# Token axis of 640 columns in place of 644, and the side taps of two convolutions in two parts

## The reference, cut to what matters

```python
def _dwconv3(u, w):
    up = jnp.pad(u, ((0, 0), (1, 1), (0, 0)))
    return up[:, :-2] * w[0] + up[:, 1:-1] * w[1] + up[:, 2:] * w[2]

def layer(l, x, cvec, ctx_kv, ang):
    h = _rmsnorm(x, norm1_g[l]) * (1 + sc1) + sh1
    q, k, v, bg, cg, xc = jnp.split(h @ w_in[l], SPLITS, axis=-1)
    ...
    y = _rmsnorm(bg * _dwconv3(cg * xc, conv_w[l]), conv_norm_g[l])
    x = x + g1 * (jnp.concatenate([o, y], axis=-1) @ w_out[l])
    h2 = _rmsnorm(x, norm2_g[l]) * (1 + sc2) + sh2
    a, b = jnp.split(_dwconv3(h2 @ w_up[l], ffn_conv_w[l]), 2, axis=-1)
    x = x + g2 * ((jax.nn.silu(a) * b) @ w_down[l])
    return x, k, v
```

## Time and profile before

| | |
|---|---|
| median of 3 runs | 1607.59 us (1606.13 to 1608.79) |
| the profiled execution's own time | 1607.43 us |
| its span, first to last instruction | 1604.9 us |
| mean granted TensorE clock | 0.989 of full speed |
| PE busy | 1563.9 us, 97% |
| DVE busy | 1029.3 us, 64% |
| ACT busy | 726.9 us, 45% |
| matmuls | 10543 |

### The profile page before, as it was taken

The page is one execution under the profiler, slowest core; times in us unless marked ns, Lnnn a source line. Parts: engine busy times, 40 slices in busy tenths (PEclk is TensorE's granted clock), DMA queues, the critical chain, the costliest instruction groups (busy, mean ns, idle before and its releaser), DMA issues. The chain is left out here.

```text
span 1604.9 us, 26306 instructions
## 1 busy us (share of the span) xinstructions
PE 1563.9 (97%) x10543; PEld 1460.1 (91%) x10543; DVE 1029.3 (64%) x1654; ACT 726.9 (45%) x1214; POOL 150.2 (9%) x174
## 2 busy tenths in 40 slices
PE   5999999999999999999989999999999999999998
PEld 4777888988999999999977788899899999999998
DVE  5672666746775865757775537576587667476673
ACT  3533454326652633526443335443465355253451
POOL 0000000002211202112000000000121120120110
PEclk9999999999999999999989999999999999999999
DMA  9555010474766947769543531034268585694862
GB/s 351 187 178 177 27 53 27 158 249 113 179 148 161 213 127 181 168 154 224 159 138 112 172 105 53 27 105 129 70 148 188 138 192 149 155 206 139 183 157 82
DMA packets 284570, 236.11 MB, mean 147 GB/s; under 512 B 10464, under 2 KB 254752, under 8 KB 284448
## 3 DMA queue, kind: packets, MB, share of 16 engines
q1 hardware_dynamic: 259920, 189.82, 37.8%
q0 software_dynamic: 23680, 44.05, 16.0%
q10 hardware_dynamic: 848, 0.56, 0.1%
HBM read 188.78 MB, written 3.67 MB: 120 GB/s over the span
## 5 line engine op out<-in xcount | busy, mean ns | idle before, releaser
L1541 ACT ACTIVATE w_hi<-raw_all 128x1024 fp32r<-128x1024 f32 x120 | 126.1, 1056 | 227.1 <-DMA raw_all<-raw_all 111.4
L1159 PE MATMUL ps<-gg,w_hi 128*128 128x322 f32 x704 | 219.1, 311 | 0.0
L1161 PE MATMUL ps<-gg,w_lo 128*128 128x322 f32 x704 | 218.7, 311 | 0.0
L1160 PE MATMUL ps<-gg,w_hi 128*128 128x322 f32 x704 | 218.4, 310 | 0.0
L2080 DVE TENSOR_TENSOR w_lo<-raw_all,w_hi 128x1024 fp32r<-128x1024 f32 x120 | 146.5, 1221 | 103.3 <-ACT w_hi L1541 102.3
L1102 PE MATMUL ps<-hc_hi,w_hi 128*128 128x322 f32 x640 | 198.9, 311 | 2.0 <-DVE ub L2103 2.0
L1104 PE MATMUL ps<-hc_lo,w_hi 128*128 128x322 f32 x640 | 199.6, 312 | 0.0
L1106 PE MATMUL ps<-hc_hi,w_lo 128*128 128x322 f32 x640 | 198.9, 311 | 0.0
L636 POOL DMA_DIRECT2D raw_all<-raw_all x160 | 136.3, 869 | 643.5 <-DMA raw_all<-in_w_up_dram 511.2
L1102 PE MATMUL ps<-ht_hi,w_hi 128*128 128x322 f32 x480 | 150.5, 314 | 3.6 <-ACT s L1559 3.5
L1975 DVE SCALAR_TENSOR_TENSOR x<-ps,modv,x 128x128 f32<-128x128 f32 (+2 forms) x240 | 90.3, 433 | 93.0 <-PE ps L1161 54.1
(11 more groups left out here) (210 smaller groups left out, 3464.0 us busy)
## 6 DMA issues: line engine op xcount, KB each, us to landing
raw_all<-in_w_up_dram SPq DMA_DIRECT2D x280, 256.0 KB, 3.8
raw_all<-raw_all POOLq DMA_DIRECT2D x160, 256.0 KB, 4.0
raw_all<-in_w_in_dram SPq DMA_DIRECT2D x48, 512.0 KB, 4.9
raw_all<-in_w_mod_dram SPq DMA_DIRECT2D x48, 512.0 KB, 4.5
raw_all<-in_w_down_dram SPq DMA_DIRECT2D x16, 768.0 KB, 4.4
raw_all<-in_w_down_dram SPq DMA_DIRECT2D x16, 640.0 KB, 4.2
mod_q<-in_w_mod_dram SPq DMA_DIRECT2D x8, 1024.0 KB, 9.4
raw_all<-in_w_out_dram SPq DMA_DIRECT2D x16, 512.0 KB, 4.3
```

What stands on the lines that cost most here:

```text
L1159: mm(out, wh[:, k, :], gh, start=k == 0, stop=False)
L1160: mm(out, wh[:, k, :], gl, start=False, stop=False)
L1161: ins = mm(out, wl[:, k, :], gh, start=False, stop=k == kf - 1)
L1541: A(whi_b[:, 2 * i:2 * (i + 1), :], src, ACT.Copy).then_inc(up_hi[i], 1)
```

## The change

T becomes 640 and HALF 320; the prompt has columns 0 to 127, the sample 128 to 639. No column is padding, so nothing is zeroed. The side taps may no longer reach over a sequence's end: each is issued as two instructions, one over the 127 inner columns of the prompt and one over the 511 inner columns of the sample.

```diff
-T = 644
+T = 640
 HALF = T // 2
-C_PROMPT, C_SAMPLE = 1, 130
+C_PROMPT, C_SAMPLE = 0, 128
+TAP_PARTS = [(C_PROMPT, SEQ - 1), (C_SAMPLE, DEC - 1)]
...
-            for a, e in ((0, 1), (C_SAMPLE - 1, C_SAMPLE), (T - 2, T)):
-                V.memset(x[:, :, a:e], 0.0)
...
-                for buf in (h_hi, h_lo):
-                    for a, e in ((0, 1), (C_SAMPLE - 1, C_SAMPLE), (T - 2, T)):
-                        V.memset(buf[:, :, a:e].bitcast(F32), 0.0)
...
-                        for j, off in ((0, 0), (2, 2)):
+                        for j, off in ((0, 0), (2, 1)):
                             dve.drain()
-                            V.scalar_tensor_tensor(out=tap[:, tile, 1:T - 1], in0=z[:, off:off + T - 2],
-                                                   scalar=cw(j), in1=tap[:, tile, 1:T - 1], op0=ALU.mult, op1=ALU.add)
+                            for c0, n in TAP_PARTS:
+                                a = c0 + 1 - off
+                                V.scalar_tensor_tensor(out=tap[:, tile, a:a + n], in0=z[:, c0 + off:c0 + off + n],
+                                                       scalar=cw(j), in1=tap[:, tile, a:a + n], op0=ALU.mult,
+                                                       op1=ALU.add)
...
-                V.memset(ps[:, B_RMS[2][0], 0:130:129], 0.0)
-                V.memset(ps[:, B_RMS[2][1], 320:322], 0.0)
...
-                    return V.scalar_tensor_tensor(out=cen[:, s, 1:T - 1], in0=u[:, s, j:j + T - 2],
-                                                  scalar=vecs[:, l, w:w + 1], in1=cen[:, s, 1:T - 1], op0=ALU.mult,
-                                                  op1=ALU.add)
+                    for c0, n in TAP_PARTS:
+                        a, b = c0 + 1 - j // 2, c0 + j // 2
+                        ins = V.scalar_tensor_tensor(out=cen[:, s, a:a + n], in0=u[:, s, b:b + n],
+                                                     scalar=vecs[:, l, w:w + 1], in1=cen[:, s, a:a + n], op0=ALU.mult,
+                                                     op1=ALU.add)
+                    return ins
```

## The result

| | before | after |
|---|---|---|
| median | 1607.53 us (13 runs, 1604.59 to 1609.88) | 1612.42 us (13 runs, 1605.48 to 1616.98) |
| profiled execution, its span | 1607.43, 1604.9 us | 1612.64, 1610.8 us |
| mean granted clock | 0.989 | 0.986 |

The ratio is 1.0026, with a 95% interval of 1.0016 to 1.0037: slower by 4.9 us, where 1604.4 and a range up to 1608.5 were forecast. The runs of after also lie further apart than those of before.

What follows compares the result with a forecast made beforehand. PE bounds the kernel through matmul count and pace. The terms -6.8 + 1.4 + 1.7 + 0.4 + 0.5 - 0.2 = -3.0 us, from 1607.43, gave 1604.4 us, with a range of 1599.5 to 1608.5.

Steps and rivals of the forecast that it cites:

- Two columns less per matmul: 7776 matmuls on PE, two columns shorter at 0.438 ns a column: 6.8 us won, bounds 6.5 and 7.2.
- The alignment rival: Row halves starting at multiples of 64 bytes make each matmul 3.6 ns shorter, 28 us in all, 1583 us; chance 0.05.
- Where that gain is not kept: At seven PE waits for snapshot s1, the gain of preceding gates is waited away: 1.4 us lost, between 0 and 2.1.
- The taps in two parts: DVE's side taps cost about 0.12 us more each, 23 us in all, mostly beside PE; it counts at four places.
- SP's block load behind `up_split_lo(g, 3)`: SP's queue waits on this DVE split before loading a later gate's block; delay behind the taps costed at nothing.
- DVE pushes the weight pipeline: Rival: the block loaded behind `up_split_lo(g, 3)` becomes what sums wait for; 6 to 11 us lost, 1609 to 1614; chance 0.10.
- Its sign in the profile: A pushed pipeline would show as ACT's DMA-sum waits growing over some 0.3 us in each third and later gate of a chunk.
- Late gates (u2): In seven late MLP gates, split taps delay snapshot u2 and PE stands still 0.3 us each: 1.7 us lost, bounds 0 and 3.
- The last gate of the chunks of five: The gated product's last low part comes about 0.1 us late, two chunks a layer: 0.4 us lost, between 0 and 0.6.
- The attention round behind the last tap: Behind the convolution group's side taps, PE's wait for probabilities grows 0.24 us, in two layers 0.5 us; bounds 0 and 1.
- The memsets: Removed zeroing on norm 1 buffers, accumulator and x, some 0.06 us each: nothing taken, at most 0.5 us won.

Runs made afterwards that it cites:

- The series of widths: Kernel before with down-projection matmuls cut by output block to 322, 322, 320, 318, 316, 304, 288 and 256 columns, addresses kept: 1595.05 us.
- The dummies: Kernel before plus two unused 62-column DVE instructions in 32 gates, ahead of `up_split_lo(g, 3)`: 1613.09 us; or behind it: 1607.5 us.
- the one with the split between the taps: Changed kernel, tensors padded to old addresses, `up_split_lo(g, 3)` moved between left and right taps in all but a chunk's first gate: 1604.95 us.
- one tap: Each tap one instruction; at 640 columns it runs across the seam between sequences: 1605.14 us at the new addresses, 1597.36 us at the old ones.
- the two runs that differ in the pads' place: Changed kernel with 128 unused bytes behind x only: 1606.41 us; with raw_all, w_hi, w_lo at changed addresses and everything behind at old ones: 1615.25 us.
- the run with pads: Changed kernel, taps in two parts, with an unused tensor behind each shortened one so every tensor keeps its old address: 1605.68 us, 0.999.
- the version with the moved split: Changed kernel with pads, the value half's last right tap put behind `up_split_lo(g, 3)` in all but a chunk's first gate: 1597.23 us, 0.9943.

## Why the prediction was wrong, by its steps

- *Two columns less per matmul*: right in kind, half the size. The term was -6.8 us with bounds of 6.5 and 7.2; the starts came 1.67 ns closer, 13 us. The series of widths gives 0.45 ns a column, the prediction's price. But rows seem to be paid by groups of 16 bytes, four columns each, and the change takes away a whole group in either half: four times 0.45 are 1.8 ns. The alignment rival had the right mechanism with too high a price (3.6 ns, 28 us). The evidence against it, equal halves at 322 columns, did not speak against it: both halves touch 81 groups.
- *Where that gain is not kept*: 1.4 us forecast, bounds 0 and 2.1. With the other two causes taken out 13 us became 10.1 by medians and 8.5 by the ratio, so about 3 to 5 us were waited away: mis-sized.
- *The taps in two parts*: exact as a cost of DVE (347 and 746 ns, eight parts in 3.78 us, 0.47 us a gate). What failed is the step that costed SP's block load behind `up_split_lo(g, 3)` at nothing. This is the rival "DVE pushes the weight pipeline", given a chance of 0.10. The dummies show the channel: 0.39 us a gate ahead of that split cost 4.9 us, behind it nothing. The taps in two parts cost 7.5 us at 644 columns and 7.3 to 8.3 at 640, so the split carries much of it, and u2 (next point) is the candidate for the rest. The argument against the rival was that PE showed only seven waits in 40 gates, so that the pipeline had reserve. PE's few waits say that it had been in time, not by how much. The prediction never measured the slack of that split. Its sign in the profile was badly chosen as well: ACT's waits for DMA sums fell, from 111.4 to 102.1 us, and over all runs but the one with the split between the taps (69.0) they lie anywhere between 82.6 and 123.1 without following the time. SP's wait for the split, 49.0 to 56.7 us, was the line to watch: it is 56.6 to 57.5 in every kernel with the MLP's taps in two parts and the split in its old place, 48.2 to 49.6 in the others that leave the split where it was, but 55.4 with the dummies ahead of it.
- *Late gates (u2)*, +1.7 us, bounds 0 and 3: the mechanism was right and too small. The list of waits has no u2 in after, but the starts show 18 late gates and 4.9 us (0.27 each, where 0.3 was forecast, in seven gates). Such stops stand in every trace with the MLP's taps in two parts, at least 10 of them, and in none with one tap, the two with dummies included. How much of them reaches the end is not shown, since a stop here shortens the next wait for s1. At 644 columns the taps in two parts cost 2.6 us more than the dummies, by medians, and their trace has 2.8 us of stops at u2.
- *The last gate of the chunks of five*, +0.4: borne out. In after, the matmul that needs the last low part starts at 692.61 and takes 0.41 us instead of 0.31, and the next one starts at 692.86, 0.10 us late. Four such places, 0.4 us together, stand in after and none in before; again the list of waits leaves them out.
- *The attention round behind the last tap*, +0.5, bounds 0 and 1: the wait shows (1.2 us in 4 times for the probabilities, 0.3 in one before), and the group takes some 1 us longer in each layer. A size too small, and within the noise of the medians.
- *The memsets*: nothing speaks for more than the nothing taken.
- *What no step had*: the shorter x moves all that is allocated behind it, and raw_all left its 256-byte boundary. This costs 4.6 us at 644 columns (ratio 1.0026) and 6.7 to 8.8 at 640 (8.8 between the two runs that differ in the pads' place, 1606.4 and 1615.3).

The account: -13 us of matmuls, +3 waited away, +8.3 for the two parts, +6.7 for the address, together +5.0; measured +4.9. This is a way to share out the difference, no test of it: -10.1 (the first two terms), +8.3 and +6.7 are the steps between four medians that begin with before and end with after, so they must add up. What tests it are the pairs that do the same thing elsewhere, and they agree within 2 to 4 us. With either cost alone the change would have been about as fast as the kernel before (1605.7 and 1605.1, ratios 0.999 and 0.9988). That the run with pads lies within the forecast's range is luck: the matmuls gained about twice what was forecast, and the taps cost about three times the 2.6 us given to them.

Left open: how the cost of the two parts divides between the split and u2; whether the 3 us waited away could be had by a faster weight pipeline; and why the runs of after scatter over 11.5 us and those of the version with the moved split over 2.4 (5 runs only). In after's 13 runs the longer spans tend to go with the lower mean granted clock (1603.7 us at 0.990, 1615.2 at 0.986; 1606.9 at 0.992), but which is the cause is not shown. The clock is not what makes after slower: its mean over the runs is 0.988, as in the runs of before that stand beside the experiments.

## What to carry to other kernels

A change of a tensor's size is also a change of the address of everything behind it: keep buffers that DMAs write on a multiple of 256 bytes, by a pad where needed, and compare the landing times of equal transfers. Where an instruction of an engine frees a buffer for a queue, ask how much slack it has before lengthening what stands ahead of it, and put it ahead of work that nobody waits for; a dummy ahead of it and one behind it tell in two runs. Few waits at the end of a chain don't show reserve in its middle. And a list of waits leaves out what is shorter than the run-out of the matmul before it: look at the distances of starts where a product begins.

## What the runs showed of the hardware that was not expected

- Equal transfers into SBUF (256 KB blocks, 2 KB a partition) land in 4.1 us instead of 3.6 to 3.9 when the target is 128 bytes off a multiple of 256, and accumulating transfers in 4.1 to 4.2 instead of 4.0 to 4.1. The whole kernel is 4.6 us slower for it at 644 columns, and 6.7 to 8.8 at 640.
- A stream of fp32 matmuls takes 1.6 to 2.8 ns more for each at 320, 288 and 256 columns if its moving rows begin 8 bytes past a multiple of 16 and so touch one group of 16 bytes more. Trimming two columns and aligning both halves gave 1.67 ns, twice the price of two columns.
- When PE's stream was stopped ahead of a product, the second matmul came about 0.25 us after the first instead of 0.147, in all 18 stops at u2 in after. A stop costs 0.10 us more than the wait itself.
- Two instructions of 0.28 us each on VectorE, in 32 gates, cost 4.9 us at one place in its queue and nothing at the next.
